# Turn 0 of the attention loop placed right behind the value tiles, and gate tiles moved one turn later

## The reference

```python
mod = silu(c) @ w_ada + b_ada
h = rms_norm(x, g_norm1) * (1 + sc1) + sh1
q, k, v, glu_a, glu_b, gate_a, gate_c = split(h @ w_in)     # widths 512 x5, 1024 x2
attn = moba_attention(rms(q), [cache_k[page_table], rms(k)], [cache_v[page_table], v]) @ w_attn_proj
u  = glu_a * sigmoid(glu_b)
cv = depthwise_causal_conv([state_conv, u], w_dwconv) + b_dwconv      # 31 taps, 512 channels
cv = silu(layer_norm(cv)) @ w_conv_proj
x  = x + gt1 * ((sigmoid(gate_a) * attn + sigmoid(gate_c) * cv) @ w_out)
x  = x + gt2 * swiglu_ffn(rms_norm(x, g_norm2) * (1 + sc2) + sh2)
```

## Time and profile before

| | us |
|---|---|
| median of 3 runs | 583.06 (583.02 to 583.2) |
| the profiled execution's own time | 585.15 |
| its span, from the first to the last instruction | 583.4 |
| mean granted clock of PE | 0.947 of full |

### The profile page before, as it was taken

The page is one execution under the profiler, slowest core; times in us unless marked ns, Lnnn a source line. Parts: engine busy times, 40 slices in busy tenths (PEclk is TensorE's granted clock), DMA queues, the critical chain, the costliest instruction groups (busy, mean ns, idle before and its releaser), DMA issues.

```text
span 583.4 us, 10394 instructions
## 1 busy us (share of the span) xinstructions
PE 525.8 (90%) x4166; PEld 443.5 (76%) x4166; DVE 395.6 (68%) x609; ACT 292.1 (50%) x519; POOL 170.2 (29%) x232
## 2 busy tenths in 40 slices
PE   4769899988979888798879999699999999999997
PEld 3558688865655646466539899599999999999996
DVE  0733584689999999989766885848565656554441
ACT  3135344486867878655464543374444444434331
POOL 8317377187777677741100000000000000000000
PEclk9689898898999999898969999889999999999999
DMA  8999548688999999989967969937466456476501
GB/s 303 371 374 339 211 164 350 246 311 300 413 388 401 420 403 420 395 332 366 378 271 271 387 242 376 367 121 261 154 215 210 146 161 162 121 195 167 153 20 38
DMA packets 82127, 159.31 MB, mean 273 GB/s; under 512 B 2572, under 2 KB 61112, under 8 KB 76951
## 3 DMA queue, kind: packets, MB, share of 16 engines
q1 hardware_dynamic: 76256, 89.27, 45.8%
q0 software_dynamic: 5120, 67.71, 28.8%
q10 hardware_dynamic: 703, 1.67, 0.8%
HBM read 156.39 MB, written 2.72 MB: 273 GB/s over the span
## 4 chain that ended last, share of the span: by engine, by line
PE 55%; DVE 21%; DMA 13%; issue 4%; ACT 4%; POOL 1%; ACTq 1%; SPq 0%; DVEq 0%; POOLq 0%
PE acc L1581 11%; PE acc L1582 11%; PE acc L1583 11%; DVE prod L1051 7%; DMA wring<-in_w_in 5%; PE acc L1453 4%; DVE sall L1058 4%; DMA wring<-in_w_ada 4%; DMA wring<-in_w_ffn_in 2%; PE acc L1466 2%; DVE wlo L1123 2%; DMA more<-in_w_ada 2%; PE acc L1468 2%; PE acc L1467 2%; PE chain L1605 2%
## 5 line engine op out<-in xcount | busy, mean ns | idle before, releaser
L1123 DVE TENSOR_TENSOR wlo<-wring,whi 128x1024 fp32r<-128x1024 f32 (+2 forms) x84 | 92.0, 1097 | 71.8 <-ACT whi L618 71.0
L618 ACT ACTIVATE whi<-wring 128x1024 fp32r<-128x1024 f32 (+2 forms) x84 | 79.9, 957 | 81.2 <-PE acc L1583 74.2
L1581 PE MATMUL acc<-xlo,whi 128*128 128x264 f32 x384 | 110.1, 287 | 0.2
L1582 PE MATMUL acc<-xhi,wlo 128*128 128x264 f32 x384 | 108.9, 284 | 0.0
L1583 PE MATMUL acc<-xhi,whi 128*128 128x264 f32 x384 | 108.8, 283 | 0.0
L573 POOL TENSOR_TENSOR cvT<-cvT,cprod 128x256 f32<-128x256 f32 x120 | 87.8, 731 | 44.6 <-ACT cprod L618 29.8
L1453 PE MATMUL acc<-hT,wring 128*128 128x264 f32 x336 | 94.4, 426 | 3.8 <-DVE hT L1011 2.0
L1453 PEld LDWEIGHTS acc<-hT,wring 128*128 128x128 f32 x336 | 64.9, 205 | 18.3 <-DMA wring<-in_w_in 3.9
L1581 PEld LDWEIGHTS acc<-xlo,whi 128*128 128x128 f32 x384 | 72.3, 188 | 1.3 <-issue 0.9
L1058 DVE TENSOR_REDUCE sall<-prod 128x32 f32<-128x2048 f32 x32 | 73.0, 2280 | 0.4
L1582 PEld LDWEIGHTS acc<-xhi,wlo 128*128 128x128 f32 x384 | 72.4, 188 | 0.0
(11 more groups left out here) (317 smaller groups left out, 915.5 us busy)
## 6 DMA issues: line engine op xcount, KB each, us to landing
wring<-in_w_ffn_in SPq DMA_DIRECT2D x22, 1024.0 KB, 7.7
wring<-in_w_ada SPq DMA_DIRECT2D x20, 1024.0 KB, 12.2
wring<-in_w_in SPq DMA_DIRECT2D x12, 1024.0 KB, 10.4
wring<-in_w_ffn_out SPq DMA_DIRECT2D x16, 704.0 KB, 5.6
more<-in_w_out SPq DMA_DIRECT2D x4, 1024.0 KB, 10.9
more<-in_w_ada SPq DMA_DIRECT2D x4, 1024.0 KB, 12.4
wring<-in_w_in SPq DMA_DIRECT2D x6, 512.0 KB, 14.3
wring<-in_w_in SPq DMA_DIRECT2D x4, 768.0 KB, 23.7
```

Of the source, the lines that this page charges most:

```text
L618: return nc.scalar.activation(out, in_, f, **kw)
L1123: v.tensor_tensor(wlo[:, place, 0:n, :], w, whi[:, place, 0:n, :].bitcast(F32), ALU.subtract)\
L1581: mm(bank[:, 0:R], whi[:, place, k - k0, :], lo[:, k, :], start=k == 0, stop=False)
L1582: mm(bank[:, 0:R], wlo[:, place, k - k0, :], hi[:, k, :], start=False, stop=False)
```

## The change

The change moves work between stages; the matmuls and their number stay the same.
- Turn 0 begins behind v3 and the head norms. PE does `ks`, the first prompt scores and the first sums right there. a0, b0, the value rows, a1 and b1 go into turn 0.
- All other tiles move about a turn later: a2, a3 and b2 in turn 1, up to g14 and g15 in turn 7 (`TURN_TILES`). Slot mix n now serves turn n + 1, and its last tile is done one turn later.
- The products and additions of the taps are 10 in turn 0, all at its end, and 22 in turns 1 to 5 (7, 7, 8).
- `gather_v(0, 0)` is issued behind v0 and not behind v3. ACT's output DMAs of k and v are issued at two places. `gated_glu(0)` moves behind `multiply_next(2)`.

```diff
+TURN_TILES = (("a0", "b0", "a1", "b1"), ("a2", "a3", "b2"), ("b3", "g0", "g1"), ("g2", "g3", "g4"), ("g5", "g6", "g7"),
+              ("g8", "g9", "g10"), ("g11", "g12", "g13"), ("g14", "g15"))
...
-         + [f"{x}{t}" for x in "qkv" for t in range(4)] + ["a0", "b0", "vn0", "vn1", "vs", "ks", "kn0", "kn1", "so", "a1", "b1"])
+         + [f"{x}{t}" for x in "qkv" for t in range(4)]
+         + ["ks", "kn0", "kn1", "so", "a0", "b0", "vn0", "vn1", "vs", "a1", "b1"])
...
-CONV_SPLIT = (6, 6, 8)
+CONV_PARTS = ((0, 0, 10),) + ((7, 7, 8),) * (CONV_LOOPS - 1)
...
@@ POOL
                     gather_k(2)
+                    gather_v(0, 0)
...
-                if name == "v3":
-                    gather_v(0, 0)
...
@@ ACT, turn b
+                    keys_out()
+                    bank = when_full(act, "so")
+                    freed(func(sown[:, :, :].rearrange("p b h -> p (b h)"), bank[:, 0:B * H], ACT.Copy), "so")
...
                 if b == 0:
-                    glu("b", 1)
...
+                    tile_out("a0")
+                elif b >= 2:
+                    tile_out(TURN_TILES[b - 1][2])
                 tap_products(b, 1)
...
-                if b < B - 1:
-                    gate(FIRST_GATE[b])
+                if b == 0:
+                    tile_out("b0")
+                    values_out()
+                    tile_out("a1")
+                else:
+                    tile_out(TURN_TILES[b][0])
...
-                if b < B - 1:
-                    gate(FIRST_GATE[b] + 1)
+                tile_out("b1" if b == 0 else TURN_TILES[b][1])
...
@@ DVE, turn b
                 if b == 0:
                     own_scores()
-                    dve.wait_ge(consts, 3)
-                    gated_glu(0)
-                    dve.wait_ge(u_ready, 1)
...
                 multiply_next(2)
+                if b == 0:
+                    dve.wait_ge(consts, 3)
+                    gated_glu(0)
+                    dve.wait_ge(u_ready, 1)
...
@@ PE
-            split("a0")
-            split("b0")
...
@@ PE, turn b
-                    split("a1")
+                    split("a0")
...
                 if b == 0:
-                    split("b1")
+                    split("b0")
+                    values_to_rows()
...
                 nc.tensor.transpose(turned_, m1, ident[:, :]).then_inc(m1t_ready, 1)
...
+                if b == 0:
+                    split("a1", k1=4)
+                else:
+                    mix = slot_ready(f"mix{b - 1}")
+                    tile(TURN_TILES[b][0], mix, 0, hT, k1=4)
...
+                if b == 0:
+                    split("b1", k0=5)
+                else:
+                    tile(TURN_TILES[b][1], mix, 1, hT, k0=5)
...
-                if b in THIRD:
-                    tile(THIRD[b], mix, 2, hT, k1=4)
+                if 1 <= b < B - 1:
+                    tile(TURN_TILES[b][2], mix, 2, hT, k1=4)
```

132 lines of the change are left out of this document (70 added, 62 removed).

## The result

| | before | changed |
|---|---|---|
| median (range, runs), us | 583.04 (582.85 to 583.2, 4) | 597.93 (596.0 to 599.62, 4) |
| ratio, 95% interval | | 1.028 (1.024 to 1.032) |
| profiled execution, span | 585.15, 583.4 | 596.0, 594.2 |
| mean granted clock of PE in it | 0.947 | 0.920 |

The change costs 14.9 us; I had forecast 3.5.

What follows compares the result with a forecast made beforehand. DVE was taken to bound the loop's eight turns. Added to the median of 583.06, +2.4 (turn 0) - 1.0 (turn 1) - 3.4 (turn 5) + 5.5 (last turn) = +3.5 gave 586.6 us; range 582.2 to 591.0, about 0.8.

Steps and rivals of the forecast that it cites:

- turn 0 starts earlier: Start of the loop: with a0, b0 and value rows moved away, `gsT` comes at 99.6 for 107.07, -7.5 us.
- wait in the middle of turn 0: Turn 0: DVE waits 4.6 us for m1's transposition, behind b0's sigmoid and the value rows; bounds 3.5 and 6.
- wait at its end: End of turn 0: DVE waits 8 us for b1's sigmoid, behind POOL's gathers, six additions and the tenth product.
- last norm to `gsT` of turn 1, with the three above: Turn 0 in sum: turn 1 starts at 135.6 for 133.15, +2.4 us (+1.0 to +3.3 by clock).
- turn 1: Turn 1 takes 24.5 us for 25.5, having less PE work ahead of it: -1.0 us (0 to -1.3).
- turns 2 to 4: Turns 2 to 4 unchanged, 0 us: POOL's extra products fit, 23.3 of 24.5 us.
- turn 5: Turn 5 falls from 27.84 to about 24.4 us as its gate weights land on time: -3.4 us.
- turns 6 and 7: Last turn: half of g13, g14 and g15 lack cover, +5.5 us (4.9 to 9), after 2.2 given back by the clock.
- the late load: Rival, turn 5: its gate weights land late again, +6.9 us, 590.0 us; chance 0.25.
- part at risk: Turn 1: V's second half leaves at 126.4 and may land late; no wait taken, 2.8 us as upper bound.
- Loads behind the loop: Rival, behind the loop: attention's and mod4's weights issued later land late, +1.5 to +4 us, 588 to 594; chance 0.09.
- The drain: Rival, ACT's table switches: four more on waits each drain about 1.38 us, 5.5 us more, 592.1; chance 1 in 100.

Runs made afterwards that it cites:

- run 5: Changed kernel with convolution products split 6, 8, 8 for 7, 7, 8 in turns 1 to 5, one fewer ahead of `pvm`: 590.8 us, ratio 1.018.
- run 9: Kernel before with only the changed kernel's convolution split, 10 products in turn 0 and 7, 7, 8 in turns 1 to 5: 589.8 us, ratio 1.013.
- run 16: Kernel before with 10 convolution products in turn 0 and 22 in turns 1 to 5, split 6, 8, 8: 583.2 us, ratio 1.004.
- run 14: Kernel before with POOL's fetch of V(0)'s second half issued later, behind its second six additions of turn 0 and K(5): 585.6 us, ratio 1.005.
- run 3: Changed kernel with b1's sigmoid ahead of the ten convolution products on ACT in turn 0: 597.3 us, ratio 1.027.
- run 13: Changed kernel with 6, 8, 8 products and, in turn 0, b1 directly behind a1 on PE, value rows behind it: 590.8 us, ratio 1.016.
- run 17: As run 13, with V's three stores on a semaphore that nothing in the loop awaits before the last turn: 585.7 us, ratio 1.012.
- run 8: Changed kernel with PE doing 5 matmuls for 20 of g13's second half, g14 and g15 in the last turn, rest left out: 599.5 us, ratio 1.033.
- run 10: Changed kernel with 6, 8, 8 products; in the last turn g13's and g14's sigmoids behind the exponential, g15 behind `psO`: 593.2 us, ratio 1.018.
- run 15: Changed kernel with 6, 8, 8 products and both last-turn edits, of run 8 (matmuls left out) and run 10 (order): 590.6 us, ratio 1.016.
- run 6: Changed kernel with 6, 8, 8 products and three quarters of the gate weights mix2 to mix6 not loaded: 591.5 us, ratio 1.019.
- run 11: Changed kernel with 6, 8, 8 products, b1's sigmoid first, V(0)'s second half used late, `values(0)` and V(1)'s fetch moved back: 594.5 us, ratio 1.023.
- run 12: As run 11, plus m1's transposition ahead of the value rows in turn 0 and the last-turn order of run 10: 593.8 us, ratio 1.020.
- run 2: Changed kernel with three quarters of the gate weights mix2 to mix6 not loaded: 600.6 us, ratio 1.031.
- run 4: Changed kernel with m1's transposition ahead of the value rows on PE in turn 0: 597.4 us, ratio 1.026.

## Why the prediction was wrong

By its own steps, traces against each other:

| step | forecast | measured |
|---|---|---|
| turn 0 starts earlier | -7.5 | -7.6 (9.25 less the 1.7 already there) |
| wait in the middle of turn 0 | 4.6 | 5.39 |
| wait at its end | 8 | 7.37 |
| last norm to `gsT` of turn 1, with the three above | +2.4 | +5.2 (38.2 to 43.4) |
| turn 1 | -1.0 | -0.8 |
| turns 2 to 4 | 0 | +4.6 (73.1 to 77.7) |
| turn 5 | -3.4 | -1.3 |
| turns 6 and 7 | +5.5 | +3.9 (43.7 to 47.6) |
| the rest | 0 | +1.0 |

The lines from the fourth on add up to 12.6; less the 1.7 us by which the changed kernel's trace was ahead at the last norm that is the 10.8 between the two traces, up to rounding.

**The step that failed** is "22 products a turn for 20 cost POOL 1.7 us, 23.3 of 24.5 with its four gathers; nothing of that is waited for until it passes the turn". I weighed the sum of POOL's work against the turn, and not its first part against what stands behind it in ACT's queue. The seventh product needs one more addition before `pvm` can be copied; PE waits 0.87 us longer for it, the mask is later, and in most of these turns PE's clock stands at its lower level for part of the time. I had put turns 2 to 4 at nothing; they took 4.6 us more in the trace, and over turns 2 to 6 the product's place measured 7.0 us (run 5's trace beside the changed kernel's). Run 5 (-5.8 us in the time), run 9 (+6.6 in the kernel before) and run 16 (4.7 of them back) show it. All seven traces with 7, 7, 8 took 130.4 to 133.3 us for turns 2 to 6, all nine with 6, 8, 8 122.7 to 127.6. It also hid turn 5's gain, for which I had only the late load as a rival.

That gain was itself read from too little. With 6, 8, 8 turn 5 took 24.55 us, as forecast; but the kernel before with other edits had its turn 5 in 24.4 (run 14) and 24.5 us (run 16) too, and run 14 had its late load in turn 4. The late load of the earlier trace rows belongs to that execution and, as far as these two traces show, not to the kernel's median, from which I took it.

**Turn 0: right mechanism, too small.** Both waits came with the right releasers and near sizes. The first was 5.39 us and not 4.6, in part since `vs` took 1.87 us for 1.04 at the lower clock (0.71 in the turn). What I had wrong lay ahead of it: from `gsT` to the reciprocal I took before's 11.1 us over, and it was 13.8, for the own scores took 1.4 us more and the mask, which PE reached only behind all of a0 at the lower clock, held DVE for 1.28. The own scores now ran while POOL was still at the last rests of the split weights (from 94.74 to 99.42, in POOL's timeline above); whether that slowed them no run tests. So b1 let POOL go 30.9 us after the last norm, where I had 28.3 and, as the upper bound, 29.1; the 126.39 beside my 125.5 looks closer only because this trace was 1.7 us ahead. I had seen the "part at risk", that V's second half would come late, took no wait for it and 2.8 us as a bound; it was 4.60 on PE. Runs 3 and 13 show that b1's sigmoid and V's second half lie side by side: each alone takes the whole gain of the start, and a third wait, for the seven stores, stood behind them. Only with all three gone or shortened (run 17) does the early start show, and then 2.8 of its 7.5 us.

**The last turn: right, somewhat too large** (+3.9 with turn 6, for +5.5). It is two ways of nearly one length, by runs 8, 10 and 15. I had expected the clock to give 2.2 us back; it did (the values' product took 3.62 us there).

**Loads behind the loop.** That rival didn't come: from the first matmul of the convolution unit to the first use of the FFN's weights (`whi`) it took 56.6 us before and 56.7 in the changed kernel.

**The drain.** A gate sigmoid of the last turn and the table load ahead of it, in ACT's timeline of the changed kernel:

```profile
302.00 1.28 ACT L626 ACT_TABLE_LOAD   x1
303.30 0.39 ACT L626 ACTIVATE gates<-acc 128x264 f32<-128x264 f32 x1
```

Here, as in the earlier trace rows, 0.02 us pass between the two. The drain of about 1.38 us that the Trainium skill adds to a switch ("ScalarE: Activation LUTs", What ACT_TABLE_LOAD costs) didn't show, and the outcome with it (592.1) had nothing behind it here.

**What adds up to 14.9.** The seventh product's place is about 7 us in turns 2 to 6: 130.4 for the 123.4 of run 5, and for the 122.7 and 123.5 that runs 16 and 14 needed without a late load in turn 5. Turns 0 and 1 are 4.0, which b1's end explains (runs 14 and 17). Turn 7 is 2.6, and what comes behind 1.0, whose cause stays open. That is 14.6, beside 14.9 in the medians; ahead of the loop the kernels don't differ beyond their spread (88.0 to 91.9 at the first head norm, in no order). That it comes so close is in part luck: it sets one trace of the changed kernel, 1.9 us below its median, against a kernel before pieced together from several traces. The same sum fails for run 17: beside the trace of before its four pieces give -2.8, -1.6, +2.6 and +0.7, and yet its median was 6.5 us above that of the kernel before on its chip, of which no trace was taken. So the causes are shown one by one, and their sizes in the median only to within a few us. No version of the changed kernel beat the one before. The best, run 17, is 1.2% (0.4 to 2.0) slower; a last turn without tiles wasn't tried with it.

## What to carry to other kernels

An engine with slack over a turn can still be late within it: before work is added to a helper engine, find the first instruction in another queue that stands behind it, and put the addition behind that. When a stage is started earlier, list all that its end waits for, buffers that are fetched into and stores included; here three waits lay side by side, so that mending one showed nothing and only the last mend paid. A late load in one profiled execution is a fact of that execution until a second trace has it.

## What the hardware showed that I had not expected

- **A short wait and a slow clock.** Where PE waited 0.50 us for `pvm` and no load was late, turns 3 and 4 ran at a granted clock of 0.93 to 1.00; where it waited 1.36 to 2.23, turns 3 to 5 of the changed kernel and of run 9 ran at 0.81 to 0.87, and were 1.3 to 3.7 us longer than with 6, 8, 8 (runs 5 and 16). Later waits in the fast turns, 1.42 and 1.02 us for DVE in run 5's turn 4, did no harm. It isn't the wait alone: in all nine traces with 6, 8, 8 PE waited 1.35 to 1.38 us for `pvm` in turn 5, and its clock was 1.00 in runs 5, 6, 11, 12, 16 and 17 (24.5 to 24.6 us), 0.93 in run 10 (25.0) and 0.81 in runs 13 and 15 (27.3). Why these differ stays open.
- **The same work moves between patterns.** Runs 2, 4 and 9 have turns 2 to 5 of 25.7, 27.3, 26.9 and 28.2 us, the changed kernel's own trace 24.5, 27.9, 25.3 and 26.5, with nearly the same waits for `pvm` in turns 3 to 5. Among the executions that the ratios count, those of one kernel lie up to 8 us apart on one chip (579.3 to 587.0 for the kernel before), and the lower times mostly go with the higher granted clocks (run 5: 588.3 us at 0.959, 595.6 at 0.931).
- **The stores were slow beside gathers.** The three stores of the value rows, 528 KB, needed 15 us beside the gathers (run 13: issued from 120.64, the last landed by 135.6). With DMA idle (changed kernel, issued from 117.52) all the traffic was over by 121: the row of rates above shows it in three slices of 0.68 us.
